# Output projection of layer 1: six of its sixteen steps placed inside the last mLSTM head, with kept partial sums and GpSimd making low weight halves

## What is computed

```python
def mlstm_mixer(xn, conv_buf, C0, n0, m0, w_in, ..., norm_w, skip, w_out):
    ...
    h, C, n, m = mlstm_chunkwise(heads(q), heads(k) * (DH_C ** -0.5), heads(v), i_pre, f_pre, C0, n0, m0)
    h = h * lax.rsqrt(jnp.mean(h * h, axis=-1, keepdims=True) + EPS)
    h = h.reshape(B, L, D_C) * norm_w.astype(F32)
    y = (h + skip * xc) * jax.nn.silu(z)
    return y.astype(xn.dtype) @ w_out, new_conv, C, n, m
...
        x = x + rmsnorm(y, p['norm_mix_post'][layer])
        xn = rmsnorm(x, p['norm_ffn_pre'][layer])
        hid = jnp.square(jax.nn.relu(xn @ p['w_ffn_up'][layer]))
        x = x + rmsnorm(hid @ p['w_ffn_down'][layer], p['norm_ffn_post'][layer])
```

## Time and profile before

| | us |
|---|---|
| median of 3 executions | 1121.28 (1120.69 to 1122.19) |
| the profiled execution | 1127.05 |
| its span, first to last instruction | 1125.3 |
| TensorE busy in it | 1068.1 (95%) |
| VectorE, ScalarE, GpSimd busy | 657.9, 529.7, 176.8 |

### The profile page before, as it was taken

One profiled execution on the slowest core, in us unless ns is written; L12 is line 12 of the kernel. 1 busy time (PEld: TensorE's weight loads), 2 busy tenths in 40 slices (PEclk: granted clock), 3 DMA queues, 4 the chain that ended last, 5 costly groups with the idle time before them and its releaser, 6 DMA issues.

```text
span 1125.3 us, 21606 instructions
## 1 busy us (share of the span) xinstructions
PE 1068.1 (95%) x8479; PEld 925.9 (82%) x8479; DVE 657.9 (58%) x963; ACT 529.7 (47%) x862; POOL 176.8 (16%) x247
## 2 busy tenths in 40 slices
PE   6999999888999999999999999999989999999995
PEld 6988778677989999998999964454528989999995
DVE  5567684622376454344897647868694385444333
ACT  5333655523456553434565453553524457553431
POOL 5124000000104220101400431300000104220100
PEclk9999999997999999999999999999989999999998
DMA  9799888997534554453744039999998534544531
GB/s 350 250 336 348 309 333 282 399 395 288 168 124 158 168 164 159 164 168 131 270 150 133 19 132 392 358 405 352 398 378 327 169 115 167 168 166 159 163 129 42
DMA packets 92761, 261.22 MB, mean 232 GB/s; under 512 B 8933, under 2 KB 10085, under 8 KB 92409
## 3 DMA queue, kind: packets, MB, share of 16 engines
q1 hardware_dynamic: 91818, 258.69, 64.4%
q0 software_dynamic: 432, 1.29, 0.4%
q10 hardware_dynamic: 432, 0.14, 0.0%
HBM read 218.36 MB, written 41.73 MB: 231 GB/s over the span
## 4 chain that ended last, share of the span: by engine, by line
PE 82%; DVE 9%; ACT 4%; issue 2%; DMA 2%; SPq 1%; DVEq 0%; ACTq 0%
PE ps L2065 21%; PE ps L2066 20%; PE ps L2067 20%; PE ps L2177 2%; PE ps L2532 2%; PE ps L2571 2%; DVE cring L1766 1%; PE ps L2557 1%; PE ps L2424 1%; PE ps L2258 1%; PE ps L2412 1%; DMA kv_b<-in_kv 1%; PE ps L2159 1%; DVE x L1311 1%; PE ps L2475 1%
## 5 line engine op out<-in xcount | busy, mean ns | idle before, releaser
L1226 DVE TENSOR_TENSOR w_lo<-w_raw,w_hi 128x1024 fp32r<-128x1024 f32 x232 | 285.3, 1236 | 221.9 <-ACT w_hi L708 221.1
L708 ACT ACTIVATE w_hi<-w_raw 128x1024 fp32r<-128x1024 f32 x232 | 242.1, 1054 | 212.5 <-PE ps L2067 177.1
L2065 PE MATMUL ps<-xin_hi,w_hi 128*128 128x288 f32 x1016 | 306.1, 301 | 13.7 <-DVE w_lo L1226 13.7
L2066 PE MATMUL ps<-xin_lo,w_hi 128*128 128x288 f32 x1016 | 303.4, 299 | 0.0
L2067 PE MATMUL ps<-xin_hi,w_lo 128*128 128x288 f32 x1016 | 303.1, 298 | 0.0
L2065 PEld LDWEIGHTS ps<-xin_hi,w_hi 128*128 128x128 f32 x1016 | 192.8, 190 | 25.3 <-DVE w_lo L1226 14.8
L2066 PEld LDWEIGHTS ps<-xin_lo,w_hi 128*128 128x128 f32 x1016 | 192.4, 189 | 0.7
L2067 PEld LDWEIGHTS ps<-xin_hi,w_lo 128*128 128x128 f32 x1016 | 192.0, 189 | 0.0
L2067 PE MATMUL ps<-hid_hi,w_lo 128*128 128x288 f32 x512 | 152.4, 298 | 0.0
L2066 PE MATMUL ps<-hid_lo,w_hi 128*128 128x288 f32 x512 | 152.3, 297 | 0.0
L2065 PE MATMUL ps<-hid_hi,w_hi 128*128 128x288 f32 x512 | 151.3, 296 | 0.0
(11 more groups left out here) (413 smaller groups left out, 1671.4 us busy)
## 6 DMA issues: line engine op xcount, KB each, us to landing
w_raw<-in_weights SPq DMA_DIRECT2D x232, 512.0 KB, 3.3
cring<-in_C SPq DMA_DIRECT2D x64, 512.0 KB, 6.4
out_Cs<-cring SPq DMA_DIRECT2D x64, 512.0 KB, 7.1
kv_a<-in_kv SPq DMA_DIRECT2D x52, 448.0 KB, 6.1
kv_b<-in_kv SPq DMA_DIRECT2D x52, 448.0 KB, 6.1
kv_w<-in_kv SPq DMA_DIRECT2D x24, 448.0 KB, 7.9
out_Cp<-cring SPq DMA_DIRECT2D x8, 512.0 KB, 6.6
out_v<-gaqkv SPq DMA_DIRECT2D x1, 1152.0 KB, 13.2
```

The source lines that it names most:

```text
L708: act.activation(w_hi[:, l % UM], w_raw[:, l % W_SLOTS], ACT.Copy).then_inc(hi_ready, 1)
L1226: dve.tensor_tensor(w_lo[:, l % W_SLOTS], w_raw[:, l % W_SLOTS], w_hi[:, l % UM], ALU.subtract).then_inc(lo_ready, 1)
L2065: pe.matmul(out, w_hi[:, j, ws], hi, start=start and kk == 0, stop=False)
L2066: pe.matmul(out, w_hi[:, j, ws], lo, start=False, stop=False)
```

## The change

The sixteen steps get a new order (`OC`, by place p), and each place has its own slots and bank. Below, step p is the one at place p of the new order. The places 0 to 5 (l = 0, 1, 2, 3, 8, 9: lower halves of six tiles) run inside the last head, one in each `chunk(3, b)` for b of 2 to 7, in banks 6 and 7. ScalarE copies each finished sum into rows of `xcc` that are no longer needed (`out_part`), and GpSimd makes the low halves of places 0 to 5. Places 6 and 7 (l = 10, 11) run behind the head, and 8 and 9 (14, 15) complete the same two tiles in their banks. Places 10 to 15 (4, 5, 6, 7, 12, 13) make the other six tiles' upper halves, and VectorE adds the kept sums in PSUM before ScalarE squares. The places 0 to 5 share three raw slots and two high slots in turn; SP loads their weights between stores, and the first two eight items earlier than before. The up-projection's raw slots are turned by two to follow on. The cut diff:

```diff
+OC = [0, 1, 2, 3, 8, 9, 10, 11, 14, 15, 4, 5, 6, 7, 12, 13]
+OC_EARLY, OC_FIRST = 6, 8
+OC_RAW = [0, 1, 2, 0, 1, 2, 0, 1, 2, 3, 4, 5, 6, 7, 0, 1]
+OC_HI = [0, 1, 0, 1, 0, 1, 2, 3, 0, 1, 2, 3, 0, 1, 2, 3]
+OC_BANK = [6, 7, 6, 7, 6, 7, 0, 1, 0, 1, 2, 3, 0, 1, 2, 3]
...
@@ SP @@
+            last = (NH - 1) * ITEMS
             for i in range(NH * ITEMS):
-                if i == (NH - 1) * ITEMS:
+                if i == last - W_SLOTS:
                     sp.wait_ge(stage_full, use(NH - 2, "vs") + 1)
-                    weights_back(0, 1)
...
+                    weights_c(0)
+                    weights_c(1)
+                if i == last:
+                    sp.wait_ge(hs_psum, NH - 1)
+                    weights_c(2)
+                if i - last in (6, 9, 12, 14, 16):
+                    n = (6, 9, 12, 14, 16).index(i - last)
+                    weights_c(3 + n, n)
                 c_store(i)
...
+            sp.wait_ge(hs_psum, NH)
+            weights_c(9)
+            sp.wait_ge(c_mm, NH * ITEMS)
+            weights_c(8, 5)
...
@@ ScalarE @@
+            def out_part(p):
+
+                act.wait_ge(step_done, STEP0[OUT_C] + p + 1)
+                act.activation(xcc[:, OC_OUT[p]], ps[:, OC_BANK[p], 0:T], ACT.Copy).then_inc(part_taken, 1)
+
+            def out_early(b):
+                if b in (2, 3):
+                    prompt_state(NH - 1, b - 2)
+                    out_part(b - 2)
+                    out_hi(b)
+                if b == 4:
+                    out_part(2)
+                if b == 5:
+                    out_hi(4)
+                    out_part(3)
+                if b == 6:
+                    out_hi(5)
+                if b == 7:
+                    out_part(4)
...
+            out_part(5)
+            out_hi(6)
             sample_roots(1)
+            out_hi(7)
             sample_high(1)
-
-            for i in (4, 5):
-                act.wait_ge(c_out[i], 16 * len(range(i, NH * ITEMS, C_SLOTS)))
-            block_out(OUT_C, 5, 2, "g_mix_post", 1)
+            out_hi(8)
+            out_hi(9)
+            for p in range(OC_FIRST, len(OC)):
+                n = p - OC_FIRST
+                if p + 2 < len(OC):
+                    out_hi(p + 2)
+                else:
+                    act_hi(p + 2 - len(OC), 0, STEP0[UP1])
+                if p + 1 == len(OC):
+                    act_hi(2, 0, STEP0[UP1])
+                act.wait_ge(step_done, STEP0[OUT_C] + p + 1)
+                if n >= 2:
+                    act.wait_ge(part_added, n - 1)
...
@@ VectorE @@
-                    if h + 1 == NH:
-                        dve_lo(0, 0, STEP0[OUT_C])
...
             sample_stats(1)
             sample_gates(1)
+            out_lo(6)
             sample_scales(1)
             sample_rows(1)
+            out_lo(7)
             sample_low(1)
-
-            steps(OUT_C, 1, lambda it, l: None)
+            out_lo(8)
+            out_lo(9)
...
+                    dve.tensor_tensor(out, out, xcc[:, OC_OUT[p]], ALU.add).then_inc(part_added, 1)
...
@@ GpSimd @@
+                else:
+                    out_lo(0)
+                    out_lo(1)
                 row_sums(h)
+            for p in range(2, OC_EARLY):
+                out_lo(p)
...
@@ TensorE @@
+                if h + 1 == NH and b >= 2:
+                    out_c(b - 2)
...
             pe.wait_ge(*made(NH * ITEMS - 2))
-            out_c(0)
+            out_c(6)
             sample_scales(1)
-            out_c(1)
...
+            out_c(7)
             pe.wait_ge(y1_ready, NH)
             pe.wait_ge(y1s_ready, 2)
-            for l in range(UM, UM * UNITS[OUT_C]):
-                out_c(l)
+            for p in range(OC_FIRST, len(OC)):
+                out_c(p)
```

More of the change, by code:

```diff
@@ L125 @@
 PIECES = [(0, 1), (1, 3), (3, 5), (5, 7), (7, 8)]
+OC = [0, 1, 2, 3, 8, 9, 10, 11, 14, 15, 4, 5, 6, 7, 12, 13]
[3 more added lines that the diff above has]
+OC_BANK = [6, 7, 6, 7, 6, 7, 0, 1, 0, 1, 2, 3, 0, 1, 2, 3]
+OC_OUT = [UM * (l // UM // 2) + l % UM for l in OC]
+TURN = OC_RAW[OC_FIRST]
+MORE = [OC_RAW.count(s) - len(OC) // W_SLOTS for s in range(W_SLOTS)]
 STOPS = (STEP0[OUT_C], STEP0[OUT_C] + 1, NSTEPS, NSTEPS + 1)
@@ L507, in loop, with raw_slot, raw_loads, oc_loads @@
                 body(n - 1)
+        def raw_slot(base, l):
+            return (l + (TURN if base >= STEP0[UP1] else 0)) % W_SLOTS
+        def raw_loads(base, it, l):
+            more = MORE[raw_slot(base, l)] if base >= STEP0[UP1] else 0
+            return 16 * (base // W_SLOTS + it + l // W_SLOTS + 1 + more)
+        def oc_loads(p):
+            return 16 * (STEP0[OUT_C] // W_SLOTS + OC_RAW[:p + 1].count(OC_RAW[p]))
         def out_bank(ph, l):
@@ L660, in _, with weights_c @@
                 c_load(i)
[L662 to L665 removed]
+            def weights_c(p, after=None):
+                if after is not None:
+                    sp.wait_ge(step_done, STEP0[OUT_C] + after + 1)
+                weights(STEP0[OUT_C] + OC[p], OC_RAW[p])
+            last = (NH - 1) * ITEMS
             for i in range(NH * ITEMS):
[L668 removed]
+                if i == last - W_SLOTS:
                     sp.wait_ge(stage_full, use(NH - 2, "vs") + 1)
[L670 to L676 removed]
+                    weights_c(0)
[6 more added lines that the diff above has]
+                    weights_c(3 + n, n)
                 c_store(i)
@@ L2052, in _, with step @@
         def _(pe):
-            def step(ph, g, l, parts, start, stop, first=None, o=None):
+            def step(ph, g, l, parts, start, stop, first=None, o=None, at=None):
                 pe.wait_ge(lo_ready, g + 1)
@@ L2066, in step @@
                     pe.matmul(out, w_hi[:, j, ws], lo, start=False, stop=False)
-                    last = pe.matmul(out, w_lo[:, l % W_SLOTS, ws], hi, start=False, stop=stop and kk == UK - 1)
+                    last = pe.matmul(out, w_lo[:, s, ws], hi, start=False, stop=stop and kk == UK - 1)
                 last.then_inc(step_done, 1)
@@ L2130, in opening @@
                         pe.matmul(out, w_hi[:, j, ws], xin_lo[:, kk], start=False, stop=False)
-                        last = pe.matmul(out, w_lo[:, j, ws], xin_hi[:, kk], start=False, stop=kk == UK - 1)
+                        last = pe.matmul(out, w_lo[:, raw_slot(base, j), ws], xin_hi[:, kk], start=False,
+                                         stop=kk == UK - 1)
                         if kk == UK - 1:
@@ L2595, in sample_scales, with out_c @@
                           start=True, stop=True, skip_group_check=True).then_inc(hs_bc, 1)
-            def out_c(l):
-                u = l // UM
-                step(OUT_C, STEP0[OUT_C] + l, l, lambda kk: (y1_hi[:, UK * (u % 2) + kk], y1_lo[:, UK * (u % 2) + kk]),
-                     u % 2 == 0, u % 2 == 1, None, OUT0[OUT_C] + UM * (u // 2) + l % UM)
+            def out_c(p):
+                if p == 0:
+                    pe.wait_ge(y1_ready, 2)
+                    pe.wait_ge(y1s_ready, 1)
+                if p < OC_EARLY:
+                    pe.wait_ge(*(reads(use(NH - 1, ("n", "mean")[p])) if p < 2 else (part_taken, p - 1)))
+                k0 = UK * (OC[p] // UM % 2)
+                step(OUT_C, STEP0[OUT_C] + p, OC[p], lambda kk: (y1_hi[:, k0 + kk], y1_lo[:, k0 + kk]),
+                     p not in (8, 9), p not in (6, 7), None, OUT0[OUT_C] + p - OC_FIRST if p >= 12 else None,
+                     (OC_HI[p], OC_RAW[p], OC_BANK[p]))
             def chunk(h, b):
```

80 lines of the change are left out of this document (60 added, 20 removed).

## The result

The changed kernel takes **1126.45 us** in the median of 17 executions (1123.10 to 1131.73); the kernel before takes 1122.23 beside it (17 executions, 1119.84 to 1126.21). The ratio is **1.0033, 95% interval 1.0021 to 1.0045**: 3.7 us slower, outside the range of 1117.2 to 1124.8 and on the other side of the forecast of 0.7 us faster.

The account below looks back on a forecast made before the run. TensorE, busy 95% of the span, was taken as the bound, so gains lay only where it waits or runs slowly. 8.9 us won against 8.2 lost made it 0.7 us faster, a median of 1120.6, range 1117.2 to 1124.8.

Parts of the forecast that it names:

- Won at the end of the head: Last head: dense steps between pairs win 7.9 us, VectorE waits 0.7 and early steps about 0.3, 8.9 us in all.
- switches: TensorE: the first matmul after another kind takes 0.40 us instead of 0.29; twelve more edges cost 1.2 us.
- the port: Head's start: VectorE's maximum with two SBUF inputs waits for GpSimd's low halves, costing 0.7 us, bounds 0 and 1.2.
- GpSimd's halves: Low halves of the early steps: 2.4 us per 128x1024 subtraction on GpSimd, costing nothing, up to 1 us if 3.4.
- The half clock: Last head's end, 836 to 847 us: TensorE's clock at 0.53; 13.4 us there would need 5.5 at full clock.
- the rival of the profile's own stretch: Last head's end: unprofiled executions keep full clock there, so 5.5 us cannot be won again; 1126.1 us, chance 0.07.
- The two pauses: Behind the head: TensorE idles 2.2 us before step 6 and 2.2 us before step 7.
- The tail: Last step: VectorE's add stands behind two low halves, so the last square and the mean come 1.9 us later.
- Falls of the clock: Rival: the new pauses lower TensorE's clock, 1.7 us per fall; one gives 1122.3, two 1124.0; two or more, chance 0.15.
- the likeliest case: Whole kernel: the sum with at most one fall of the clock, 1118.9 to 1122.9 us, chance 0.42.
- SP's queue, transfers: Weight loads moved among stores: enough cover, 3.0 us at step 4's weight, so no cost.
- From the profile to the median: Whole kernel: the profiled execution's 5.8 us above the median carried over, turning 1124.6 into 1120.6 us.

Follow-up runs that it names:

- the version with both repairs: Changed kernel with VectorE's kept-sum add before the low half, and high half 6, low halves 6 and 7 made earlier: 1116.43 us, ratio 0.9948; another chip 0.9947.
- The filled variants: Changed kernel with 14 and 13 dead matmuls in the pauses before steps 6 and 7, the second also 20 before the last square: ratios 1.0009 and 1.0028.
- the two variants: Changed kernel with the kept-sum add moved ahead of the low half, ratio 0.9999; changed kernel storing half of each last-head state tile, ratio 1.0032.
- its variant: Kernel before with ten dead matmuls ahead of the outer products of the last head's pairs 6, 7 and 8: 1123.97 us, ratio 0.9992.
- halved stores: Changed kernel storing only half of each state tile of the last head, 4.5 MB less: 1126.32 us, ratio 1.0032.

## Why the prediction was wrong

The stretch in the traces, in us, from 4 profiles of before, 5 of the change and 2 of the version with both repairs: 104.3, 105.7 and 97.1. Term by term:

- **Won at the end of the head.** Predicted 8.9, less 1.2 for switches and 0.7 for the port: 7.0. From the group sum to the end of the last step the kernel before takes 98.2 us in the mean, of which 0.3 is the fall near 800 that one of its four profiles has. The filled variants, which have the change's pauses and no fall, take 94.1, with 4.4 of pause in it. So 8.2 were won. Each pair with its step does go back to back (a step takes 3.37 with both its edges, as forecast), GpSimd's halves take 2.40 us as forecast (though the rows of 0.73 and 1.29 us that the forecast came from are additions and not, as it says, subtractions), and the port costs TensorE 0.24, or nothing, instead of 0.7. But the cause was only half right. **The half clock was worth nothing like 5.5 us there**: without it the old stretch takes nearly as long, because VectorE paces it. The change wins by giving TensorE steps to do in that time. This is also why the rival of the profile's own stretch, 1126.1, landed near the measurement by chance: its reason fell.
- **The two pauses.** Predicted 2.2 + 2.2, measured 2.29 + 2.11. Right.
- **The tail.** Predicted 1.9, measured 3.1 (892.93 to 896.65 is 3.72, before it was 0.66). This is one step that failed. The times of the last add behind add 14 were right (4.6 us against 4.53), but add 14 was taken to be on time. Steps 10 to 15 had been costed as single additions and not as a ring through two engines, whose 3.47 us are longer than a step.
- **Falls of the clock.** This is the other step that failed. Predicted: none in the sum, at most one in the likeliest case (0.42), two or more 0.15, at 1.7 us each. Measured against the filled variants: two falls in the pauses, 3.1 us together, in two profiles of the change's five (four of seven with the two variants), and one behind the last square in all five, for 0 to 0.6 us. That is 1.4 us in the mean of the five. The other three have the fall near 800 instead, at 1.7 us, which is not the change's own. The kernel before has as many falls, but most of them at the end of its head, where VectorE sets the pace; the sum over all executions fits, 16.3 us of clock missing before and 16.6 after. I had entered half clock as time won and had not charged it as a cost where TensorE becomes the bound.

8.2 won against 4.4 + 3.1 + 1.4 lost is 0.7 us slower; 0.7 more is the draw of the fall near 800, which three of the change's five profiles have and one of the four before. Together this is the 1.4 that the means of the stretch say (105.7 - 104.3, standard error 0.7). The times say 3.7 (2.4 to 5.1), so some 2 us stay open. They are not behind the stretch: there the profiles of the change take 219.3 to 219.4 us, three of the kernel before 219.0 and one 220.5. They are not ahead of it either: the group sum starts at 799.1 us in the mean of the thirteen profiles that hold the change, and at 799.5 in the five of the kernel before and its variant. What the runs do show is that for all eight kernels that hold the change the ratios say more time, against the kernel before, than the stretches do, by 0.1 to 4.2 us and 1.7 in the mean. All eight are compared with the same four profiles. If these are long by that much (102.6 in place of 104.3, where the shortest seen is 103.2), the gap closes, and the won part falls to about 6.5, near the 7.0 predicted. This is an estimate from those means; no profile shows it.

- **SP's queue, transfers.** As predicted: no wait of TensorE for a transfer, and halved stores gain nothing.
- **From the profile to the median.** The difference of 5.8 us between the profiled execution and the median was carried over as a constant. It was the place of one execution in a spread of some 7 us, much of it from clock falls in other stages: over the profiles here the same instructions ahead of the stretch end anywhere from 795.4 to 802.9. The two that end first (795.4 and 795.6) lost 5.1 us of full clock ahead of it; all that lost 10.2 end at 799.5 or later.

## What to carry to other kernels

Price a half-clock stretch by what the other engines do in it: where another engine sets the pace, the clock is worth little, and where a change makes TensorE the bound, each short pause costs its length and, in some executions, a fall on top. When an evacuation gets a second instruction on another engine, add up the ring that returns to the same engine and compare it with the step; a ring 10% too long shows as a wait only at its end. Before a partial result is parked to fill a gap, see what the first steps behind the gap wait for: here a new order of a few instructions on two engines turned 1.0033 into 0.9947.

## What the runs showed of the hardware

- The falls of the granted clock in these rows lose 1.7 us of full clock each, near 800, in the pauses, or behind the last square; the one at the old head's end loses two or three times as much. A pause of 2.1 to 2.3 us between dense steps brought one in four profiles of seven, a wait of 0.93 us none in three, and the wait of 2.96 us one in nine of nine.
- GpSimd's subtraction of 128x1024 (fp32r out of two f32) takes 2.40 us, twice VectorE's 1.22. While two of them ran, VectorE's maximum with two inputs in SBUF took 1.29 us instead of 0.42, and beside a later one its subtraction for y_lo 1.97 instead of 1.22; its updates that read PSUM kept their 2.47 for two, and its reciprocal its 1.75. The Trainium skill (SBUF — State Buffer, section "Who interferes with whom") says that a VectorE instruction with two SBUF inputs contends with a GpSimd one that reads SBUF, and that one with at most one SBUF input, outside the modes that use both ports, does not. The trace agrees.
- One profiled execution is one draw. Ahead of the changed code, in identical instructions, profiles differ by up to 7.5 us, and a comparison of two profiles gave the wrong sign here.
